# Four output-projection rows of the second token block issued inside the dilated attention's rounds

## The reference, cut to what matters

```python
def dilated_mixture(q, k, v, rel_bias):
    outs, lses = [], []
    for g, (window, dil) in enumerate(DIL_PAIRS):      # (128, 1), (512, 4), (2048, 16)
        o, l = dilated_group(q[:, :, g], k[:, :, g], v[:, :, g], tab, window, dil)
        ...
    wts = jax.nn.softmax(jnp.stack(lses, 0), axis=0)
    return jnp.sum(wts[..., None] * jnp.stack(outs, 0), axis=0)

def sb_dilated_mixer(h, w_in, rel_bias, w_out):
    ...
    y = jnp.concatenate([oc, od], axis=-1) @ w_out     # oc: 512 columns, od: 256 columns
    return y.astype(h.dtype)

x = layer_norm(RES_ALPHA * x + (1.0 + g_m) * y, ln_g[layer, 0], ln_b[layer, 0])
hf = x * (1.0 + sc_f) + sh_f
yf = swiglu(hf, ffn_w1[layer], ffn_w3[layer], ffn_w2[layer])
```

## Time and profile before

| what | value |
|---|---|
| median of 3 runs | 1331.03 us (1327.98 to 1331.96) |
| the profiled execution, its own time | 1334.0 us |
| its span | 1332.2 us, 16978 instructions |
| TensorE busy | 1293.3 us (97%) |
| VectorE, ScalarE, GpSimd busy | 642.1 us (48%), 475.4 us (36%), 505.8 us (38%) |
| mean granted TensorE clock | 0.991 |
| the dilated rounds | about 897 to 921 us of the span |
| output projection of layer 1 | about 921 to 955 us of the span |

### The profile page before, as it was taken

One profiled execution on the slowest core, in us unless ns is written; L12 is line 12 of the kernel. 1 busy time (PEld: TensorE's weight loads), 2 busy tenths in 40 slices (PEclk: granted clock), 3 DMA queues, 4 the chain that ended last, 5 costly groups with the idle time before them and its releaser, 6 DMA issues.

```text
span 1332.2 us, 16978 instructions
## 1 busy us (share of the span) xinstructions
PE 1293.3 (97%) x6486; PEld 1079.4 (81%) x6486; DVE 642.1 (48%) x851; ACT 475.4 (36%) x683; POOL 505.8 (38%) x207
## 2 busy tenths in 40 slices
PE   7999999999999999999999899999999999999996
PEld 6878877789888888888887677888898888888884
DVE  5489746868543534410457766667781011110005
ACT  3443344633313232211342456535442222322222
POOL 0243322423535353544234223322354444444444
PEclk9999999999999999999999899999999999999998
DMA  9971636630655554873136522231122322234312
GB/s 330 187 157 66 221 107 116 223 109 20 234 188 190 185 193 161 271 121 96 63 116 237 150 79 64 75 116 48 53 100 92 104 94 94 94 96 146 102 52 63
DMA packets 93538, 173.61 MB, mean 130 GB/s; under 512 B 15735, under 2 KB 62087, under 8 KB 93356
## 3 DMA queue, kind: packets, MB, share of 16 engines
q1 hardware_dynamic: 90344, 169.43, 42.4%
q10 hardware_dynamic: 3140, 3.43, 1.0%
HBM read 170.68 MB, written 4.52 MB: 132 GB/s over the span
## 4 chain that ended last, share of the span: by engine, by line
PE 82%; DVE 7%; issue 5%; POOL 2%; DMA 1%; ACT 1%; SPq 0%; POOLq 0%; DVEq 0%; ACTq 0%
PE ps L1179 14%; PE ps L1180 14%; PE ps L1181 14%; PE ps L1211 6%; PE ps L1209 6%; PE ps L1210 6%; POOL w_lo L714 2%; PE ps L1613 1%; PE ps L1615 1%; PE ps L1614 1%; PE ps L1363 1%; PE ps L1317 1%; PE ps L1318 1%; PE ps L1319 1%; DMA ada_raw<-astream 1%
## 5 line engine op out<-in xcount | busy, mean ns | idle before, releaser
L714 POOL TENSOR_TENSOR w_lo<-raw,w_hi 128x1024 fp32r<-128x1024 f32 x191 | 475.1, 2495 | 784.6 <-ACT w_hi L772 780.7
L1179 PE MATMUL ps<-h_lo,w_hi 128*128 128x512 f32 (+2 forms) x1064 | 398.2, 374 | 3.4 <-DVE h_lo L2287 2.2
L1181 PE MATMUL ps<-h_hi,w_lo 128*128 128x512 f32 (+2 forms) x1064 | 394.7, 371 | 0.0
L1180 PE MATMUL ps<-h_hi,w_hi 128*128 128x512 f32 (+2 forms) x1064 | 394.7, 371 | 0.0
L772 ACT ACTIVATE w_hi<-raw 128x1024 fp32r<-128x1024 f32 x198 | 208.3, 1056 | 483.9 <-DMA raw<-wstream 159.2
L1179 PEld LDWEIGHTS ps<-h_lo,w_hi 128*128 128x128 f32 (+1 forms) x1064 | 201.3, 189 | 41.7 <-issue 4.9
L1181 PEld LDWEIGHTS ps<-h_hi,w_lo 128*128 128x128 f32 (+1 forms) x1064 | 201.1, 189 | 34.9
L1180 PEld LDWEIGHTS ps<-h_hi,w_hi 128*128 128x128 f32 (+1 forms) x1064 | 201.2, 189 | 33.5
L2406 DVE TENSOR_TENSOR tmp<-tmp,ps 128x512 f32<-128x512 f32 x44 | 30.1, 687 | 267.1 <-PE ps L1181 265.3
L1209 PE MATMUL ps<-w_hi,hid_lo 128*128 128x512 f32 x336 | 130.9, 390 | 0.0
L1211 PE MATMUL ps<-w_lo,hid_hi 128*128 128x512 f32 x336 | 130.7, 389 | 0.0
(11 more groups left out here) (297 smaller groups left out, 1620.0 us busy)
## 6 DMA issues: line engine op xcount, KB each, us to landing
raw<-wstream SPq DMA_DIRECT2D x205, 512.0 KB, 4.2
ada_raw<-astream SPq DMA_DIRECT2D x80, 512.0 KB, 4.4
ada_first<-astream SPq DMA_DIRECT2D x16, 256.0 KB, 6.8
ada_first<-astream SPq DMA_DIRECT2D x8, 512.0 KB, 10.3
ln_rows<-row_scratch SPq DMA_DIRECT2D x3, 1024.0 KB, 6.8
skew_scratch<-f_scratch ACTq DMA_DIRECT2D x1, 2304.0 KB
xa<-xT SPq DMA_DIRECT2D x4, 512.0 KB, 8.6
out<-xa SPq DMA_DIRECT2D x3, 512.0 KB, 3.5
```

The costliest lines, as they stand in the source:

```text
L714: nc.gpsimd.tensor_tensor(w_lo[:, slot, :], raw[:, slot % RAW, :], w_hi[:, slot, :].bitcast(F32), ALU.subtract).then_inc(sem("w_lo_ready"), 1)
L1179: pe.matmul(o, w_h, x_l, start=start, stop=False)
L1180: pe.matmul(o, w_h, x_h, start=False, stop=False)
L1181: return pe.matmul(o, w_l, x_h, start=False, stop=stop)
```

## The change

Token block 2's rows with chunks 0, 1, 2 and 3 are issued among the rounds: one before the first turn, one behind the first three turns, one behind round 4 and one behind round 7. What follows block 1 is then only chunks 4 and 5 of block 2. The wait for all four banks in front of the turns becomes a wait for each bank. On VectorE the subtractions for chunks 0 to 3 are spread (0 and 1 around the copy of `vd`, 2 behind copy 1, 3 behind copy 3), and each reciprocal is made in two halves of 256 columns: the first behind copy n = 5, 9 or 13, the second, with the product, behind copy n = 7 or 11, or after the loop. On ScalarE the rounded part of the fourth projection slot moves from before the copies to behind copy 0.

```diff
 # ScalarE
         dil_exp(0, 0)
         dil_exp(0, 1)
-        hi_until(OUT[1] + RING)
         for n in (0, 2, 4, 6, 8, 10, 12, 14, 15):
...
             if n // 4 + 1 < 4:
                 dil_exp(n // 4 + 1, n % 4 // 2)
+            if n == 0:
+                hi_until(OUT[1] + RING)
             if n == 10:
                 hi_of_chunk(H_BASE["cat1"] + 4, 4)
 # TensorE
-        wait_free(pe, "vd0")
+        def early_row(k):
+
+            slot_waits(OUT[1] + k)
+            pe.wait_ge(sem("h_ready"), H_BASE["cat1"] + k + 1)
+            out_row(1, 2, k)
+
+        assert pair("vd0") == 0 and pair("vd0+") == 2
+        pe.wait_ge(sem("nm_ready"), 1)
+        early_row(0)
+        for n in range(3):
+            pe.wait_ge(sem("v_dve" if n % 2 else "v_act"), 7 + n // 2)
+            turn_round(n)
+        early_row(1)
         wait_free(pe, "vd0+")
-        for n in range(3):
-            turn_round(n)
         for n in range(16):
             pv_round(n)
             if n + 3 < 16:
                 turn_round(n + 3)
+            if n in (4, 7):
+                early_row(2 if n == 4 else 3)
...
-        pe.wait_ge(sem("nm_ready"), 1)
-        for k in range(6):
+        for k in (4, 5):
             m = out_row(1, 2, k)
         m.then_inc(sem("y_full"), 1)
         turn(2, 0)
 # VectorE
+        lo_of_staged(0)
         v_blocks("vd0", (3,))
+        lo_of_staged(1)
+
+        def dil_rec(h, half):
+
+            r, t = 64 * (h % 2), slice(256 * half, 256 * half + 256)
+            dve.wait_ge(sem("pv_done"), 4 * h + 4)
+            if h and half == 0:
+                dve.wait_ge(*((sem("dil_out"), h // 2 + 1) if h % 2 else (sem("h_tmp_ready"), H_BASE["cat1"] + 5)))
+            return V.reciprocal(rec[r:r + 64, t], ps[64 - r:P - r, 6 + h % 2, t])
...
-            dve.wait_ge(sem("pv_done"), 4 * h + 4)
             if h % 2 == 0:
                 tmp_free(e)
-            if h:
-                dve.wait_ge(*((sem("dil_out"), h // 2 + 1) if h % 2 else (sem("h_tmp_ready"), H_BASE["cat1"] + 5)))
-            link(V.reciprocal(rec[r:r + 64, :], ps[64 - r:P - r, 6 + h % 2, :]))
+            link(dil_rec(h, 1))
...
             if n in (1, 3):
-                for q in (n - 1, n):
-                    lo_of_staged(q)
+                lo_of_staged(n // 2 + 2)
             if n == 13:
                 lo_of_chunk(H_BASE["cat1"] + 4, 4)
             if n % 4 == 1 and n >= 5:
+                dil_rec(n // 4 - 1, 0)
+            if n % 4 == 3 and n >= 7:
                 dil_out(n // 4 - 1)
+        dil_out(2)
+        dil_rec(3, 0)
         dil_out(3)
```

## The result

| | before | changed |
|---|---|---|
| median of 20 executions each | 1331.07 us | 1336.0 us |
| their range | 1326.68 to 1336.05 | 1332.39 to 1340.22 |
| ratio, 95% interval | | 1.004 [1.0031, 1.0049] |
| the profiled execution, its span | 1334.0, 1332.2 | 1339.76, 1338.0 |
| TensorE busy, mean granted clock | 1293.3 us, 0.991 | 1295.4 us, 0.989 |

The change makes the kernel 0.4% slower, 4.9 us by the medians; forecast were 5.1. What follows shows where they lie.

A forecast was written before the change was run, and what follows sets the result against it. TensorE, busy 97% of the span, was taken as the bound. Rows 5.4 + switches 0.6 - filled stalls 3.9 + new stall 0.8 = +2.9 us, plus 2.2 for the clock, gives +5.1: 1336.1 us, range 1332.2 to 1339.6.

The forecast's parts named there:

- The forecast case: Behind the rounds: chain late by about 2.9 us and clock low behind the idle stretch, 1334 to 1338 us; chance 0.55.
- the chain: VectorE's residuals and ScalarE's scaling, 11.0 us from block 0's end, set the turn's start; +2.9 us, bounds +1.5 and +6.0.
- the clock: At the turn and block 3's first row: TensorE's granted clock falls to 1.2 GHz after idling; +2.2 us, bounds 0 and 3.4.
- The rows: Before the last value round: four early rows of 1.36 us each take +5.4 us of TensorE's time.
- The switches: At each early row: changing from small to large matmuls and back costs 0.15 us, +0.6 in all, bounds 0.0 and 1.0.
- the new stall: Before round 12: TensorE waits for ScalarE's copy 12, late because head 1's product stands behind copy 11; +0.8 us, bounds 0 and 2.
- What they fill: In the rounds: the early rows and halved reciprocals remove TensorE's old stalls; -3.9 us, bounds 0 and -3.9.
- The hole: In front of the turn, behind block 2's last rows: TensorE stands idle for 5.6 us.
- The other moves, at nothing: Fourth slot's rounding behind copy 0, chunk 3's subtraction beside GpSimd, VectorE's longer tail, two extra slots: no cost.
- A: Behind block 2: the clock isn't lowered or its low stretch falls into idle time; only +2.9 us, 1334.0; chance 0.25.
- B: In front of the turn: the residual chain doesn't hold it, filled stalls count in full; -2.5 us, 1328.5; chance 0.08.
- C: In the rounds: the rows fill little as VectorE becomes late elsewhere; up to +6.0 and the clock's 2.8, 1339.8; chance 0.12.

The follow-up runs named there:

- e1: The changed kernel with four throwaway rows (24 matmuls) issued in front of the turn; 1332.0 us, ratio to before 1.0019.
- e6: e3 with ScalarE's h_hi of chunk 4 behind copy 12 instead of before it; 1329.69 us, ratio to before 0.9989.
- e3: The changed kernel without the four early rows, all six rows of block 2 behind block 1 again; 1329.46 us, ratio to before 0.9994.
- e4: The changed kernel with only rows 0 and 1 early, rows 2 and 3 back before rows 4 and 5; 1332.05 us, ratio to before 1.0014.
- e5: The changed kernel with each reciprocal in one piece again, its product right behind copies 5, 9 and 13; 1333.85 us, ratio to before 1.0026.
- e2: The changed kernel with four rows of block 3 in front of the turn instead of behind it; 1330.95 us, ratio to before 1.0001.
- e8: e7 with rows 0 and 1 of block 2 issued early; 1329.17 us, ratio to before 0.9987.
- e7: e6 with all six rows of block 0 in front of those of block 1; 1329.46 us, ratio to before 0.9989.
- e10: e8 with one row of block 3 (chunk 2) in front of the turn; 1326.07 us, ratio to before 0.9961.
- e11: The changed kernel with block 0 first, chunk 4's h_hi behind copy 12, four block 3 rows before the turn; 1327.7 us, ratio to before 0.9977.
- e9: The changed kernel with std_of(2) in front of the FFN's first weight slot on ScalarE; 1335.71 us, ratio to before 1.0034.

## Why the prediction was right

**The forecast case came in, with both of its terms.** Predicted was +2.9 for the chain and +2.2 for the clock; the traces show +2.56 and, by e1 against the changed kernel, +2.29.

*The rows.* 1.36 us each was right. The switches were oversized: 0.15 a row was taken, and rows 2 and 3 show 1.40 - 1.36 = 0.04. That is 0.4 us too much in the sum. Against it the new stall, with the restart behind it, was 0.15 us more than its 0.8. The two together explain the 2.9 against 2.56.

*What they fill.* All four old stalls went, as the walk through the rounds said. *The new stall* was 0.8 in the walk; it is 0.67 of marked idle time, and 0.84 between starts (919.16 to 920.43, 1.27 instead of 0.43), at the named round and with the named releaser. e6 took its cause away, and of e3's 1.23 us 0.18 were left.

*The hole.* 5.6 us forecast, 5.5 measured. The chain takes what it took: from the start of residual 0 to the end of block 1's scaling 10.75 us before, 10.74 after. One thing was overlooked: the turn also waits for residual 1's sum (`r_ready`), so a single transpose of block 0 splits the hole. It changes nothing in the sum.

*The clock.* It fell in the hole and came back behind the turn, as in the nearest row of before. The value taken was the middle between two rows, and it was partly luck that it fits this well. By e4 and e5 the price is 1.5 to 1.6 where the low clock covers 3.1 to 3.4 us of work, so one and the same hole costs 1.5 to 2.3 us. The upper bound of 3.4 has no row behind it: the dearest row gives 2.8.

*The other moves, at nothing.* Chunk 3's subtraction took 1.92 us beside GpSimd (the forecast had it meet GpSimd), and the copy behind it was in time. The halves were put down at no price on TensorE, and the product's new place was priced by itself. But the two are one edit, and e5 undoes it: 0.93 us come back, the whole of the new stall and its restart. So the sentence that the halves serve the old stalls was right only without rows 2 and 3 (e3, e4); with these in place, whole reciprocals are in time. A slip without effect: chunk 5 is wanted after nine rows, not ten; the time, 936, is right.

**The rivals.** A (the clock stays) is refuted by the trace: the low level ran through the turn. B (no cover needed) is refuted by the idle stretch in front of the turn and by e2. C (little filled) is refuted by the rounds themselves. The rule of the Trainium skill (TensorE: Matmul & The Clock Gate, Part 4: PE-mode transpose), that the full clock doesn't engage for transposes, is not borne out: in e5 the clock came back at about 948.1, and since 945.00 TensorE had run nothing but transposes; the first large matmul starts at 948.11. In the changed kernel the turn did run low from end to end, and the clock rose behind it, at 953.9, as that rule would have it. But the price was 2.29 us and not the upper bound that the prediction drew from the rule.

## What to carry to other kernels

Work that is moved out of a place leaves a place. Before moving matmuls into a stall, look at what they covered where they stood: here eight rows (10.9 us, the last two of block 1 and the six of block 2) hid an 11.0 us chain on two other engines, and moving four of them lengthened the kernel by all that they did not fill, with a lowered clock on top. By these runs two rows, as many as the first two stalls hold, were worth moving only with the start of the covered chain brought forward first (e4: 1.94 us later than before; e8: 0.66 us earlier than e7, which the ratios can't tell). It also pays to look in the in-order list of each engine for a step that waits in front of something urgent (e10).

## What had not been expected

- A hole of 2.66 us in front of the turn was enough to lower the clock, and it cost 1.6 us (e4). After the 5.5 us hole the price was 2.3 us in one execution and 1.5 in another (e5). A longer hole was not dearer in proportion. Holes of 0.80 us (e8) and 0.86 us (e11) left the clock at 1.00.
- The cover in front of the turn did not do away with the low clock: in e2 a stall of 1.90 us behind the turn lowered it for 3.4 us there. Throwaway matmuls in the hole itself did (e1): 24 more, 2.29 us less.
- A single weight slot in front of `std_of(2)` was worth next to nothing in the changed kernel (e9), but a row of block 3 in front of the turn, which also frees that slot's place early, was worth over 1 us in e10 against e8 (`half_chunks` -3.11 against -2.05). What a link in a chain is worth depends on whether TensorE is late by the same amount for a reason of its own.
